# Two-layer hybrid backbone in fp32 on one core: row tiles of the norms reordered, modulation between late weight splits, adaLN sums three tiles behind

## The reference, cut to what matters

```python
for layer in range(2):
    mod_lat = jnp.split(silu(c) @ ada_w[layer] + ada_b[layer], 6, axis=-1)      # six rows of 1024
    mod_ctx = jnp.split(silu(c_ctx) @ ada_w[layer] + ada_b[layer], 6, axis=-1)
    h = rms_norm(x, pre_mix_g) * (1 + mod[1]) + mod[0]
    y = attention(h @ w_in) @ w_out
    x = x + mod[2] * rms_norm(y, post_mix_g)
    h = rms_norm(x, pre_ffn_g) * (1 + mod[4]) + mod[3]
    u = h @ w_up; gate, val = u[:, :2816], u[:, 2816:]
    f = (gelu(conv3(gate)) * val) @ w_down
    x = x + mod[5] * rms_norm(f, post_ffn_g)
```

## Time and profile before

| | |
|---|---|
| Median of 3 runs | 1861.03 us (1859.75 to 1861.37) |
| The profiled execution | 1856.1 us, span 1854.4 us |
| PE busy | 1706.3 us (92%) |
| DVE, ACT, POOL busy | 1019.9, 645.6, 267.3 us |
| Chain that ended last | PE 80%, DVE 6%, DMA 4%, ACT 3%, issue 3% |
| Mean granted TensorE clock | 0.972 |

### The profile page before, as it was taken

One profiled execution on the slowest core, in us unless ns is written; L12 is line 12 of the kernel. 1 busy time (PEld: TensorE's weight loads), 2 busy tenths in 40 slices (PEclk: granted clock), 3 DMA queues, 4 the chain that ended last, 5 costly groups with the idle time before them and its releaser, 6 DMA issues.

```text
span 1854.4 us, 27146 instructions
## 1 busy us (share of the span) xinstructions
PE 1706.3 (92%) x10042; PEld 1366.3 (74%) x10042; DVE 1019.9 (55%) x1927; ACT 645.6 (35%) x1089; POOL 267.3 (14%) x396
## 2 busy tenths in 40 slices
PE   5898898989989999999996969998989799999998
PEld 1876565668878888888785857885667598888886
DVE  3656455754657777776653482156743634443445
ACT  2424455653321212212223332235643433233343
POOL 0414222320200000000010030125521200000001
PEclk9999999999989999999998989998999899999999
DMA  8479441114514343344254542354502523332233
GB/s 300 162 256 322 77 106 44 24 38 158 172 46 121 106 136 116 111 136 126 70 126 116 173 153 96 130 154 104 139 10 80 158 70 90 91 109 72 80 125 136
DMA packets 258270, 224.21 MB, mean 121 GB/s; under 512 B 67484, under 2 KB 218411, under 8 KB 258178
## 3 DMA queue, kind: packets, MB, share of 16 engines
q1 hardware_dynamic: 249156, 202.50, 36.3%
q0 software_dynamic: 7008, 18.79, 3.5%
q10 hardware_dynamic: 2016, 1.71, 0.3%
HBM read 193.71 MB, written 29.25 MB: 120 GB/s over the span
## 4 chain that ended last, share of the span: by engine, by line
PE 80%; DVE 6%; DMA 4%; ACT 3%; issue 3%; SPq 2%; POOL 2%; ACTq 0%; DVEq 0%
PE ps L1171 29%; PE ps L806 10%; PE ps L808 10%; PE ps L807 10%; PE ps L993 5%; PE ps L1075 4%; PE ps L1038 4%; PE ps L1181 1%; DMA w_raw<-in_ffn_down 1%; PE ps L1030 1%; PE ps L863 1%; PE ps L1045 1%; ACT arena L1425 1%; PE ps L1155 1%; DMA wide_raw<-in_ada_w 1%
## 5 line engine op out<-in xcount | busy, mean ns | idle before, releaser
L806 PE MATMUL ps<-w_hi,act_hi 128*128 128x512 f32 (+2 forms) x952 | 370.1, 389 | 21.8 <-DVE act_lo L1614 18.6
L1614 DVE TENSOR_TENSOR w_lo<-w_raw,w_hi 128x2048 fp32r<-128x2048 f32 (+3 forms) x114 | 209.5, 1838 | 310.7 <-ACT w_hi L1316 310.7
L808 PE MATMUL ps<-w_hi,act_lo 128*128 128x512 f32 (+2 forms) x952 | 366.2, 385 | 0.0
L807 PE MATMUL ps<-w_lo,act_hi 128*128 128x512 f32 (+2 forms) x952 | 366.2, 385 | 0.0
L1316 ACT ACTIVATE w_hi<-w_raw 128x2048 fp32r<-128x2048 f32 (+3 forms) x110 | 172.4, 1568 | 308.3 <-PE ps L808 249.2
L1171 PE MATMUL ps<-act_lo,w_hi 128*128 128x512 f32 (+1 forms) x912 | 278.3, 359 | 0.0
L1171 PE MATMUL ps<-act_hi,w_hi 128*128 128x512 f32 (+1 forms) x912 | 277.1, 358 | 0.0
L1171 PE MATMUL ps<-act_hi,w_lo 128*128 128x512 f32 (+1 forms) x912 | 274.6, 355 | 0.0
L806 PEld LDWEIGHTS ps<-w_hi,act_hi 128*128 128x128 f32 x952 | 180.9, 190 | 62.1 <-issue 23.3
L808 PEld LDWEIGHTS ps<-w_hi,act_lo 128*128 128x128 f32 x952 | 180.3, 189 | 34.4
L807 PEld LDWEIGHTS ps<-w_lo,act_hi 128*128 128x128 f32 x952 | 180.6, 190 | 33.5
(11 more groups left out here) (129 smaller groups left out, 2008.2 us busy)
## 6 DMA issues: line engine op xcount, KB each, us to landing
arena<-in_ada_w SPq DMA_DIRECT2D x44, 1024.0 KB, 9.3
w_raw<-in_ffn_up SPq DMA_DIRECT2D x88, 512.0 KB, 5.1
w_raw<-in_ffn_down SPq DMA_DIRECT2D x88, 256.0 KB, 3.0
w_raw<-in_odd_w_in SPq DMA_DIRECT2D x20, 512.0 KB, 4.9
arena<-mods SPq DMA_DIRECT2D x16, 512.0 KB, 7.3
proj_odd<-arena POOLq DMA_DIRECT2D x26, 256.0 KB, 2.7
x_after_mix<-arena SPq DMA_DIRECT2D x10, 512.0 KB, 2.9
arena<-x_after_mix SPq DMA_DIRECT2D x10, 512.0 KB, 5.0
```

The lines of the kernel that those rows point to most:

```text
L806: mm(out_, s_hi, m_hi, start=start, stop=False)
L807: mm(out_, s_hi, m_lo, start=False, stop=False)
L808: return mm(out_, s_lo, m_hi, start=False, stop=stop)
L1614: V.tensor_sub(out_, full, hi.bitcast(fp32)).then_inc(sem_, 1)
```

## The change: order of row tiles, of modulation, of sums and of loads

1. **Norms (1 to 3).** The loops of PE, ACT and DVE are replaced by written lists. DVE: gate 0, add 0, gate 1, add 1, then scale and shift of both, and so on. PE transposes tiles 0, 1, 2 after pieces 12, 15 and 19 of down0's end (before: after 15, 21, 23), after 6, 7, 9 of out0's last unit pair (before 7, 10, 11) and tiles 0 and 1 after 5 and 6 of out1's (before 7 for tile 0, and tile 1 by itself). The first pieces of up0, up1 and in1 are reordered too: unit 0's first. POOL's order stays.
2. **Modulation.** DVE multiplies the gains between the splits of unit 18 and of unit 19 of down0 (down1), not behind 19. The gains have a home in unused columns of Y and are loaded at the start of the second half of down. x is loaded ahead of in1's weights.
3. **Sums.** In up0, tile j multiplies round j-2 and collects round j-3; tiles 0 and 1 have none. PE sums no round ahead of tile 2 of the up projection. Five rounds (19 to 23) are left for down0, one after each two units; their loads stand between SP's trips. `toeplitz` is written after the store of round 19.

```diff
-        IN1_START = [("turn", 3), (0, 0), (0, 1), (0, 2), (1, 0), ("turn", 4), (1, 1), (1, 2), ("turn", 5), (0, 3), (1, 3)]
+        TURNS_OUT = {NT: (6, 7, 9), LT: (5, 6)}
+        TURNS_DOWN = (12, 15, 19)
+            if name in ("norm2", "norm4"):
+                return Y[:, 2 * n:2 * n + 2, 512:1024]
+            return h_tok[n].rearrange("p (a c) -> p a c", a=2)
...
                     if layer == half == 0:
-                        sp.wait_ge(t_free, ada_round(1, FT - 3) + 1)
-                        ada_unit(1, FT - 1, 1)
-                        for k in range(2):
-                            run_loop(sp, 1 + 2 * k, 3 + 2 * k, down_trip)
-                            sp.wait_ge(t_free, ada_round(1, FT - 2 + k) + 1)
-                            ada_unit(1, FT + k, k)
+                        for i in range(5):
+                            if i:
+                                down_trip(i)
+                            sp.wait_ge(t_free, ada_round(1, FT - 5 + i) + 1)
+                            ada_unit(1, FT - 3 + i, (FT - 3 + i) % 2)
                     else:
+                        if half:
+                            if layer == 0:
+                                sp.wait_ge(ada_summed, ADA_UNITS)
+                            gain_loads(nf)
...
                 mod_loads(nf)
+                sp.wait_ge(g_lo, base(f"down{layer}", "g") + 17)
+                x_moves(nf, range(2))
...
-                sp.wait_ge(g_lo, base(f"down{layer}", "g") + FT)
-                gain_loads(nf)
-                x_moves(nf, range(2))
...
-                if full:
-                    ada_across(base(name, "t"), 0, 1)
-                run_loop(pe, 1, FT // 2 - 1, lambda i: [tile(i, k, True) for k in range(2)])
+                for k in range(2):
+                    tile(1, k, True)
+                run_loop(pe, 2, FT // 2 - 1, lambda i: [tile(i, k, True) for k in range(2)])
...
                         if ada == 1:
-                            ada_multiply(k, i + (ADA_USES + 1))
+                            ada_multiply(k, i + ADA_USES)
...
+                if layer == 0:
+                    for n in range(11):
+                        step(0, 0, n, 0 if n < 9 else None)
+                        if n % 2 == 0:
+                            ada_next(FT - 3 + n // 2)
...
-                modulation(("norm2", "norm4")[layer])
+                    if n == 18:
+                        modulation(("norm2", "norm4")[layer])
...
-            run_loop(pool, 0, FT // 2 - 1, lambda i: [ada_store(1, i * 2 + (T0 + 2 + k), k, i * 2 + (2 + k))
+            run_loop(pool, 0, FT // 2 - 2, lambda i: [ada_store(1, i * 2 + (T0 + 2 + k), k, i * 2 + (2 + k))
```

More of the change, by code:

```diff
@@ L1140, in rows_product @@
                         turned(nm, t)
-                    for half in range(2):
+                    for half in halves:
                         b = 3 * j + 2 * half if g < 2 else 3 * j + 1
@@ new lines, in norm @@
+                act.wait_ge(g_lo, base(name, "g"))
+                if not h:
+                    for t in range(T):
+                        square_y(t)
+                    return
+                square_y(0)
+                square_y(1)
+                square_x(0)
+                square_x(1)
+                if T == NT:
+                    square_y(2)
+                    turned_hi(0)
+                    square_x(2)
+                    turned_hi(1)
+                    square_y(3)
+                    square_x(3)
+                    late(0)
+                    turned_hi(2)
+                    square_y(4)
+                    square_y(5)
+                    turned_hi(3)
+                    square_x(4)
+                    late(1)
+                    square_x(5)
+                else:
+                    late(0)
+                    turned_hi(0)
+                    square_y(2)
+                    turned_hi(1)
+                    square_y(3)
+                    late(1)
+                    square_x(2)
+                    square_x(3)
@@ L1359, in first_half @@
+                turned_hi(T - 2)
+                turned_hi(T - 1)
             def first_half(t):
@@ new lines, in scale, with shift, split @@
+                def scale(q):
+                    dve.wait_ge(rs_x, H0 + q + 1)
+                    if q >= 3:
+                        dve.wait_ge(t_done, T0 + 2 * (q - 3) + 2)
+                    scale_h(name, q, x_new[q % 2], h_tok[q % 3])
+                def shift(q):
+                    shift_h(name, q, h_tok[q % 3])
+                def split(q):
+                    split_h(name, q)
+                gate(0)
+                add(0)
+                gate(1)
+                add(1)
+                if not h:
+                    for t in range(2, T):
+                        gate(t)
+                        add(t)
+                    return
@@ new lines, in norm @@
+                scale(0)
+                shift(0)
+                scale(1)
+                shift(1)
+                if T == NT:
+                    gate(2)
+                    split(0)
+                    add(2)
+                    split(1)
+                    gate(3)
+                    add(3)
+                    scale(2)
+                    shift(2)
+                    scale(3)
+                    shift(3)
+                    split(2)
+                    late(0)
+                    gate(4)
+                    add(4)
+                    split(3)
+                    gate(5)
+                    add(5)
+                    late(1)
+                else:
+                    split(0)
+                    late(0)
+                    gate(2)
+                    split(1)
+                    add(2)
+                    gate(3)
+                    add(3)
+                    late(1)
@@ L1748, in finish @@
+                scale(T - 2)
+                shift(T - 2)
+                scale(T - 1)
+                shift(T - 1)
+                split(T - 2)
+                split(T - 1)
             def finish(layer, c, x, t):
```

217 lines of the change are left out of this document (107 added, 110 removed).

## The result

| | before | changed |
|---|---|---|
| Median of 4 runs | 1860.39 us | 1826.87 us (1824.68 to 1827.21) |
| Ratio to before | | 0.9813 (95% interval 0.9801 to 0.9826) |
| The profiled execution | 1856.1 us | 1824.7 us, span 1823.0 us |
| Mean granted clock | 0.972 | 0.979 |

A forecast was written before the change was run, and what follows sets the result against it. PE, busy for 92% of the span, was taken as the bound. Terms 0 + 10.5 + 4.6 - 0.2 + 16.1 + 3.5 = 34.5 us less gave 1821.6 us profiled, 1826.5 for the median; range 1809 to 1843.

The forecast's parts named there:

- Norm1, forecast 0: Around norm1: between a gain of 4.1 us and a loss of 3, taken as 0.
- Start of up0, -10.5: Start of up0: PE's 9.1 us wait for `ada_sum` and 1.4 us of slow clock behind it go.
- Start of down0, -4.6: Start of down0: the 3.0 us wait and its 1.6 us of clock go, the sum lagging three tiles.
- Inside down0, +0.2: Inside down0: the `toeplitz` write moves behind round 19's store; PE's stop is 14.6 us instead of 14.4, clock unchanged.
- two stops: Inside down0, by the cited rule: PE stops at two units in a row; 32.5 us less in all, median 1828.5.
- Norm2, -16.1: Around norm2: idle time and clock fall from 24.3 us to 8.2, with earlier gains and the modulation rows binding instead.
- Norm3, -3.5: Around norm3: stops of about 5.6 and 2.1 us with two clocks of 2.0, 11.7 in all, remain.
- A: Rival in down0: the collision of loads with `toeplitz` costs more, stop 26 us instead of 14.6, time 1838; chance 0.14.
- B: Rival in down0: `toeplitz` nearly misses the weight loads, stop of 3 us, time 1815; chance 0.12.
- C: Rival at norm2 and norm3: bound by the per-tile chain, not order; 12 of 19.6 us stay, 1838.5; chance 0.16.
- D: Rival in up0: DVE's growth past 2.7 us slack delays PE 18 times; at 6 us per tile 1886; chance 0.04.
- E: Rival at the start of down0's second half: stops only move, a new one of some 34 us, 1861; chance 0.02.

The follow-up runs named there:

- the first experiment: The changed kernel timed and profiled again with no edit: 1830.45 us, ratio 0.9814 to the kernel before.

## Why the prediction was right, point by point

The median was forecast as 1826.5 and measured as 1826.9. That close it is by luck: of its terms norm1 was 3.9 us and norm3 2.1 too small, down0 with norm2 2.4 too large, and 6.7 us of stretches that it had at nothing went against it; of 34.5 us the profile shows 31.4.

- **Norm1, forecast 0: it gained 2.6 us in this execution.** Its idle time was 3.0 us and is 3.0 (2.7 and 0.3). The step counted 2.1 of the 3.0 before; the waits of the kernel before in that stretch have one line more:

```profile
PE ps L1155 <- DVE w_lo L1614: 1.0, 1, 1.0
```

  The clock price of the stop that is left was nothing, in the second profile 1.6, and the one of before was 2.6, not 2.0; the step took one price for every stop from rows at down0. That its order comes to 5 to 7 us when it is put back is due to the first rows of up0, which go with it and belong to the next term.
- **Start of up0, -10.5: right.** The 9.1 us and 1.4 to 1.6 of clock went; tiles now follow without a slow one:

```profile
525.06 33.92 PE ps L1189 x192
```

  192 matmuls in 33.92 are 16.96 us a tile, where the first had 18.56. The step named both parts of the cause, though its first sentence reads as if the lag of the sums did it all: the cover of some 12 us measured 11.4, and the stop of 2.8 without it 2.86. By the runs the lag alone leaves 2.9 of the 9.1 us, the order alone 3.4. From out0 to down0 the rows give 9.1, 1.6, norm1's 2.6 and 0.6 ahead of down0's first unit, 13.9 of the 14.4.
- **Start of down0, -4.6: right.** The 3.0 us are back when the sums are.
- **Inside down0, +0.2, measured about +3.** The mechanism was right, the same collision at the ninth unit, some 29 us earlier in the program. On POOL's timeline:

```profile
906.15 0.54 POOL L2187 DMA_DIRECT2D mods<-late_row  x1 [23.77 <-DVE late_row L1701]
...
913.41 2.81 POOL L2315 DMA_DIRECT2D toeplitz<-rpb  x1 [0.30 <-POOL rpb L2313]
```

  With down0's start moved by 10 us this is 916.2 and 923.4 on the clock of before, against 916.7 and 922.4 forecast. PE's stop began where it was forecast, 952.3 by that clock for 952.1. It ended at 959.40, 969.4 by that clock, against 966.7. Off was the end: the write was issued 1.0 us later than forecast, and from its issue to PE's next matmul it took 46.0 us, where it was 43.9 before and the forecast had 44.3. The write itself is 0.4 of that; 1.7 stand behind its landing (7.1 us for 5.4), as the last load of the unit that PE wanted landed 2.6 us behind the write. The same 2.3 us for the place, whatever the write's length, stand between the other kernels (the first experiment). The loads of two units were caught:

```profile
DMA to landing us min/median/max: 19.5/24.6/28.1
```

  There was one stop only: unit 7's two loads, issued at 913.0 and 913.4, landed within 2.6 and 3.3 us, and the four loads caught, of the next two units, landed about the write's end (951.9 to 956.2, the write at 952.3). The rule that the prediction cites from the Trainium skill ("DMA: Bandwidth & Descriptors", section "Queues, rings and completion order"), that a semaphore write lands only after every earlier write of the same DMA engine, had been read as holding unit 7's load too, with two stops. The trace does not bear out that reading. That the caught loads landed only with the write agrees with the rule, but the trace does not tell it from a mere lack of turns on the engines.
- **Norm2, -16.1: right, nearly by its steps.** Adds of tiles 0 and 1 come 4.42 us apart where 4.4 was worked out; the stops are 1.4 for 1.8, 2.8 for 2.9, and small ones. By idle time and clock it is 24.3 less about 7. Of that the early gains, with x, are worth 10 by their run, the order 7.4. The move ahead of unit 19's split, which the step took along for the price of its stop, gains nothing by itself.
- **Norm3, -3.5, measured -5.6.** The stops came as 2.1 and 4.7, for 2.1 and 5.6, with one clock price for two.
- **The rivals.** A came in part: the stop grew to 17.1 us, and was 20.7 in the changed kernel's second profile, where A had 26 (its sign was over 20, which the second profile and every later one with the whole write in down0 show). What lengthened it is the write's own duration more than the loads beside it. B asked for a stop of 3, C for powers and stops at norm2 as before, D for waits in up0 from tile to tile, E for a new wait at down0's second half; none is in the trace.

## What to carry to other kernels

A wait names the last instruction of a chain: the 9.1 us for a sum were a chain of 14.6 us on ACT and DVE with 5.6 us of PE's work to cover it. Giving the chain less to do and giving it more cover each took some 6 us off, and only runs with each edit put back by itself, and then both, told that apart. An engine that ends a wait need not have been late: DVE had stood idle for 11 us ahead of that chain. A large transfer that must be written some time held up the weight loads beside it here for as long as it lasted. Cut into parts of 0.48 MB in the attention it cost nothing that shows, in up0 3 to 5 us; whole it stopped PE for 14 to 22 us where it met weight loads, and cost 5 in the attention.

## What the hardware showed beside that

A stop of 2.7 us left TensorE's granted clock at 1.00 in one execution, and the same stop in the same program was followed by 0.57 over 4 us in another. One of 2.8 us elsewhere took it to 0.57, and two of 2.1 and 1.0 us close together to 0.50. Neither the length of a stop nor its place in the program told by itself what it cost.

The same write of 3.8 MB took 38.5 and 38.9 us to land in the first profiles of the two kernels and 42.3 to 46.1 in down0 on the three later occasions, and the stop of PE behind it went from 14.4 and 17.1 to 20.3 to 21.7 us with it. The kernel before was 4 us slower there too (1864 to 1865 us for 1860).
